# Three transformer blocks in one kernel: beta folded into the delta rule's decay, and each attention as one loop

## The chip, the cores and the metric

The kernel runs on one core of one Trainium2 chip. The metric is the device time of one launch in microseconds. All data and all matrix products are fp32.

## The reference, cut to what matters

Sequence 512, model width 1024, one batch. The first block mixes with a gated delta rule and a spatial gating unit, and then runs a mixture of 16 experts. The second block has two layers, each an attention (a forget-gate attention called FOX, then a latent attention with rotary keys called MLA) and a mixture of experts.

```python
# gated delta rule, 8 heads of 128
k_beta, v_beta = k * beta, v * beta
decay = where(causal, exp(g_cum[t] - g_cum[s]), 0)
a_mat = where(strict, (k_beta @ k.T) * decay, 0) + eye
u = solve(a_mat, v_beta)
w = solve(a_mat, k_beta * exp(g_cum))
v_new = u - w @ state
out   = (q * exp(g_cum)) @ state + ((q @ k.T) * decay) @ v_new
state = state * exp(g_last) + (k * exp(g_last - g_cum)).T @ v_new
# attention, 16 heads; cum only in FOX (head width 64), MLA has width 96 for q and k, 64 for v
s = q @ k.T * scale + cum[t] - cum[s]          # causal mask
o = softmax(s) @ v
# c @ w_ada: one row times 1024 x 6144, for each of the two layers
```

## The kernel before, in words

The program is a row of stages. A stage is a block: each engine has its own list of instructions in it, and the next stage begins when all engines and the queue of SP have come to the end of theirs. Inside a stage the engines wait for each other by named steps (`PE.wait(act, "sums")`: ScalarE waits until TensorE has done the step `sums`). There are 128-row tiles of the sequence, `T` = 4 of them, and 8 banks of PSUM of 512 fp32 columns.

Weights come through a ring of four SBUF slots (`Weights`), issued by SP in the order of use; a slot is loaded again when TensorE has finished with it. Beside the stages of the first block VectorE also sums `c @ w_ada` in *slabs*: SP loads 128 rows of `w_ada` (512 KB) into one of four buffers, VectorE multiplies and adds them into a 128 x 1024 accumulator, and after each 8 slabs SP stores the sum. `take_slabs` gives a stage its share. `project` (L343) is a general product stage: 8 jobs of 8 matmuls, the result of each drained by VectorE, with `slabs` spread evenly behind the jobs (`after`, L353). Its call at L796 (the product with `w_sgu_out`) has the last 12 slabs of a layer, so SP waits at its end for the last store.

The stage at L588 to L678 first multiplies the sequence by the 16 columns for a and b (L596 to L600: 4 tiles x 8 matmuls of 16 columns), then runs 16 jobs of the product for u and v. VectorE normalises q and k meanwhile, and ScalarE and VectorE make beta and the decay rate g from a and b.

The delta rule (L800 to L1030) works on chunks of 128 tokens, four rounds. In each round TensorE makes cumulative sums of g (`sums`), transposes q, k and k*beta (`qT`, `kT`, `kbT`), half of a product for the gate z, then `kk` (k against k*beta) and `qk`, the levels of a blockwise inverse of the unit triangular matrix (`t0`, `lev`, `dinv`, `turn`), and the products with the state. GpSimd makes k*beta and v*beta and k*decay. VectorE makes the differences of g for the decay (`diff`, `clip`), copies the identity into `inv_t` (`eye`), drains `kT`. ScalarE takes the exponentials and drains `qT` and `kbT`.

`attention` (L1977) is called for FOX (L2367) and MLA (L2741). For each group of 8 heads it has two stages: one that transposes all q and k of the group (64 transposes, L2006; ScalarE and VectorE take them to SBUF, L2013 and L2019), and the loop over 32 units (head h, tile t) in which the scores S (L2071), the transposes of the exponentials (L2079) and the products with v (L2089) run interleaved with lags of 3 and 4 units. In FOX the negative cumulative log-forget is a further row of the transposed keys, against a row of ones in q: it is transposed in the stage before (`cumT`, L2222 and L2298) and moved there by one DMA for each head (L2040), and rows 64 to 95 are padded. The row sums of the softmax come from the exponential's accumulator (L2102). After both groups `transpose_stage` (L254) turns the output. Bank use in the loop: four for S, two for the turned exponentials, two for the output.

Of the kernel before, what the change touches and what calls it, by code (L numbers as in the profile page):

```python
# [116 lines left out]
def build(nc, D, OUT, stop=None):  # L117
# [19 lines left out]
    with ctx:  # L137
# [205 lines left out]
        def project(srcT, kblocks, widths, by, drain, mids=0, slabs=0, first=None):  # L343
# [9 lines left out]
            after = lambda j: beside[j * slabs // len(jobs):(j + 1) * slabs // len(jobs)]  # L353
# [226 lines left out]
        a_in, g_all, beta_all, tmp_a, tmp_b = (sc[:, 288 + 32 * i:288 + 32 * (i + 1)] for i in range(5))  # L580
        ssq = [buf[6][:, 2304 + 32 * i:2304 + 32 * (i + 1)] for i in range(2)]
        square = [buf[6][:, 0:DM], buf[6][:, DM:2 * DM]]
        def th(a):
# [6 lines left out]
                    ["dt", "neg", "low", "high", "rate", "g"] + [("unit", i, t) for t in range(T) for i in range(2)])  # L590
        ac_names = ["beta", "exp", "rate"] + [(s, i) for i in range(2) for s in ("log", "inv")] + ["log"] + [("drained",) + j for j in jobs]
        stage(["ab"] + [("sum",) + j for j in jobs], ac_names, dv_names + slab_names(beside))
        with nc.Block() as block:
            @block.tensor
            def _(pe):
                for t in range(T):  # L596
                    for k in range(KD):
                        last = nc.tensor.matmul(bank[0][:, t * 2 * H:(t + 1) * 2 * H], featT[:, k, t * P:(t + 1) * P],
                                                ab_w[:, k, :], start=(k == 0), stop=(k == KD - 1))
                PE.done(last, "ab")  # L600
                for j, (n, t) in enumerate(jobs):
# [7 lines left out]
                    PE.done(last, ("sum", n, t))  # L609
                    if t == T - 1:  # L610
                        W.mark_used(ids[n], PE.sem, PE.value(("sum", n, t)))

            @block.vector
            def _(dve):
# [12 lines left out]
                AC.wait(dve, "beta")  # L627
                DV.done(nc.vector.tensor_tensor(th(a_in), ab[:, :, 0:H], bcast(dt_bias.unsqueeze(1), P, T, H), ALU.add), "dt")
# [24 lines left out]
            def _(act):  # L653
                ab = bank[0][:, 0:T * 2 * H].rearrange("p (t n) -> p t n", t=T)
                PE.wait(act, "ab")
                AC.done(nc.scalar.activation(th(beta_all), ab[:, :, H:2 * H], ACT.Sigmoid), "beta")
                nc.scalar.preload_act_table_set("natural_log_exp_and_others")
                DV.wait(act, "low")
# [144 lines left out]
        qkbT = buf[3][:, 0:2048].rearrange("p (h i n) -> p h i n", h=H, i=2)  # L803
        kT, decT = heads(buf[3][:, 2048:3072]), heads(buf[3][:, 3072:4096])
        qk, negT, inv_t, inv = (heads(buf[5][:, i * DM:(i + 1) * DM]) for i in range(4))
        lev, kb0, kd, vnew = (heads(buf[4][:, i * DM:(i + 1) * DM]) for i in range(4))
        kbs = [kb0, heads(ring[2][:, 0:DM])]
        gcol, gtot = sc[:, 448:456], sc[:, 456:464]
        e_g, e_tot, e_rest, b_eg = (sc[:, 464 + 8 * i:472 + 8 * i] for i in range(4))
# [6 lines left out]
        pe_n = (["sums", "qT", "kT", "kbT", "z"] + [("kk", u) for u in units] + [("qk", h) for h in halves] + [("t0", u) for u in units] +  # L816
                [(s, l, h) for l in LV for s in ("lev", "dinv") + (("turn",) if l < NL - 1 else ()) for h in units] +
                [(s, h) for s in ("ks", "qs") for h in halves] + [("vn", h) for h in halves] + [(s, h) for s in ("o", "s") for h in halves])
        ac_n = (["g", "e", "rest", "decay", ("qT", 0), ("qT", 1), ("kbT", 0), ("kbT", 1), "z"] + [("t0", u) for u in units] +
                [(s, l, h) for l in LV for s in ("lev",) + (("turn",) if l < NL - 1 else ()) for h in units] + [("vn", h) for h in halves])  # L820
        dv_n = (["rest", "beg", ("diff", 0), ("diff", 1), "clip", "eye", ("kT", 0), ("kT", 1)] + [(s, u) for u in units for s in ("neg", "first")] +
                [("qk", h) for h in halves] + [("add", l, h) for l in LV for h in units] +
                [(s, h) for h in halves for s in ("rk", "r")] + [(s, h) for h in halves for s in ("oq", "o", "sg", "s")])
        po_n = ["kb", "vb", "kd", "causal"]
# [7 lines left out]
        with nc.Block() as block:  # L832
            @block.tensor
            def _(pe):
# [6 lines left out]
                for c in range(T):  # L841
                    g_c = g_all[:, c * H:(c + 1) * H]
                    kb = kbs[c % 2]
# [29 lines left out]
                    for h in halves:  # L873
                        for j in range(HH):
                            last = nc.tensor.matmul(bank[5 + h][:, j * P:(j + 1) * P], kT[:, HH * h + j, :], qkbT[:, HH * h + j, 0, :], start=True, stop=True)
# [1905 lines left out]
```

## Time and profile before

| | |
|---|---|
| runs | 2282.35 us median of 3 (2280.46 to 2284.82) |
| profiled execution | 2285.79 us, of which the span of the trace 2283.8 us |
| TensorE matmul busy | 2138.2 us, 94% of the span |
| VectorE, ScalarE, GpSimd busy | 919.9, 525.1, 141.7 us |
| mean DMA rate | 164 GB/s |

Times in rows are microseconds from the start of the span unless marked ns. A row of the timeline has start, duration, engine, line of the kernel, operation, what it writes and reads, how many instructions were merged into the row, and in brackets the idle time of the engine just before and what ended it. An fp32 matmul is two instructions in the trace, a transpose is one. A releaser like "PEq L358" is the sequencer at a stage's boundary. The duration of a merged row runs to the last result, about 0.16 us after the engine could take the next instruction.

### The profile page before, as it was taken

What the parts mean: (1) busy time and instruction counts of PE and PEld (TensorE: products, weight loads), DVE (VectorE), ACT (ScalarE), POOL (GpSimd) and SP (SyncE); (2) the same over time, 40 slices, a digit from 0 to 9 for tenths busy, and PEclk for the clock granted to TensorE, in tenths of its full rate; (3) what the DMA queues carried; (4) which work ended last, traced back from release to release, by engine and by line L of the source; (5) the groups of instructions that cost most, each with busy time, mean ns of one, the idle gap of its engine ahead of it and who ended that gap; (6) DMA issues with size and microseconds to landing.
All of it is one profiled execution on the core that took longest, in us unless ns stands there. A gap on an engine that the chain in (4) does not pass through costs nothing. (4 is left out here: it accounts for less than half of the span.)

```text
span 2283.8 us, 21392 instructions
## 1 busy us (share of the span) xinstructions
PE 2138.2 (94%) x8144; PEld 1229.1 (54%) x8144; DVE 919.9 (40%) x1687; ACT 525.1 (23%) x1244; POOL 141.7 (6%) x201
## 2 busy tenths in 40 slices
PE   7999999989999999999799989999998989999994
PEld 4445445478884445444345468554444567654442
DVE  2446246344554024212355656342233467532223
ACT  1111011034332001111231146220003446411000
POOL 1000000011102000100100010000001000001001
PEclk9998999999999998999899999989998999989997
DMA  5333475420013224799626820149994120046995
GB/s 168 96 89 110 116 244 192 157 48 1 1 38 92 74 94 147 259 383 379 254 72 236 313 103 1 32 145 319 379 361 170 58 95 1 3 147 232 370 367 209
DMA packets 205258, 374.30 MB, mean 164 GB/s; under 512 B 21737, under 2 KB 123353, under 8 KB 204897
## 3 DMA queue, kind: packets, MB, share of 16 engines
q1 hardware_dynamic: 88080, 174.17, 23.4%
q10 hardware_dynamic: 105696, 157.30, 19.5%
q0 software_dynamic: 11376, 41.42, 4.8%
q8 instruction: 67, 1.10, 0.2%
q14 instruction: 39, 0.31, 0.0%
HBM read 329.31 MB, written 43.52 MB: 163 GB/s over the span
## 5 line engine op out<-in xcount | busy, mean ns | idle before, releaser
L1536 PE MATMUL bank<-ring,work 128*128 128x512 f32 x768 | 343.3, 601 | 11.4 <-issue 7.1
L1536 PEld LDWEIGHTS bank<-ring,work 128*128 128x128 f32 x768 | 144.1, 193 | 177.4 <-issue 177.4
L1547 PE MATMUL bank<-ring,work 128*128 128x512 f32 x384 | 173.0, 593 | 4.0 <-DVE work L1561 4.0
L2236 PE MATMUL bank<-ring,featT 128*128 128x512 f32 x384 | 170.8, 606 | 4.2 <-ACT featT L1925 2.6
L522 PE MATMUL bank<-featT,ring 128*128 128x512 f32 x384 | 168.7, 593 | 1.0 <-PEq L244 1.0
L1279 PE MATMUL bank<-ring,work 128*128 128x512 f32 x384 | 166.5, 593 | 3.1 <-PEq L244 3.1
L1558 DVE TENSOR_TENSOR work<-work,bank 128x256 f32<-128x256 f32 x48 | 20.2, 421 | 300.4 <-ACT work L1555 300.4
L2236 PEld LDWEIGHTS bank<-ring,featT 128*128 128x128 f32 x384 | 74.3, 195 | 96.0 <-issue 94.2
L1279 PEld LDWEIGHTS bank<-ring,work 128*128 128x128 f32 x384 | 72.3, 190 | 91.2 <-issue 91.2
L522 PEld LDWEIGHTS bank<-featT,ring 128*128 128x128 f32 x384 | 71.2, 190 | 82.0 <-issue 82.0
L608 PE MATMUL bank<-ring,featT 128*128 128x512 f32 x256 | 112.9, 605 | 0.0
L370 PE MATMUL bank<-ring,work 128*128 128x512 f32 x256 | 110.3, 593 | 2.0 <-PEq L697 1.0
L1547 PEld LDWEIGHTS bank<-ring,work 128*128 128x128 f32 x384 | 69.5, 190 | 74.9 <-issue 74.9
L1555 ACT ACTIVATE work<-bank 128x256 f32<-128x256 f32 x48 | 18.4, 383 | 394.5 <-PE bank L1536 394.5
L2071 PE MATMUL bank<-work 96*128 96x128 f32 (+3 forms) x256 | 96.2, 467 | 9.4 <-DMA work<-work 6.1
L1068 PE MATMUL bank<-ring,featT 128*128 128x512 f32 x192 | 85.0, 602 | 3.6 <-PEq L832 3.6
L2089 PEld LDWEIGHTS bank<-work,featT 128*128 128x128 f32 x640 | 81.5, 192 | 10.1 <-ACT featT L2102 8.1
L2089 PE MATMUL bank<-work,featT 128*128 128x64 f32 x640 | 86.5, 266 | 0.3
L1712 POOL DMA_INDIRECT work<-x_rows,ismall x48 | 45.1, 941 | 653.7 <-PE bank L1531 417.1
L608 PEld LDWEIGHTS bank<-ring,featT 128*128 128x128 f32 x256 | 49.7, 195 | 62.4 <-issue 62.4
L370 PEld LDWEIGHTS bank<-ring,work 128*128 128x128 f32 x256 | 48.5, 190 | 63.2 <-issue 63.2
L1566 DVE TENSOR_TENSOR work<-bank,work 128x512 f32<-128x512 f32 x64 | 41.2, 685 | 89.7 <-PE bank L1547 89.7
(426 smaller groups left out, 2928.6 us busy)
## 6 DMA issues: line engine op xcount, KB each, us to landing
ring<-in_w_in SPq DMA_DIRECT2D x16, 2048.0 KB, 13.3
ring<-in_moe_w_gate ACTq DMA_DIRECT2D x28, 1024.0 KB, 8.7
ring<-in_moe_w_up ACTq DMA_DIRECT2D x28, 1024.0 KB, 11.4
ring<-in_moe_w_down ACTq DMA_DIRECT2D x28, 1024.0 KB, 10.1
ring<-in_w_ada SPq DMA_DIRECT2D x48, 512.0 KB, 6.6
y_rows<-work ACTq DMA_DIRECT2D x48, 512.0 KB, 9.9
ring<-in_expert_w_gate ACTq DMA_DIRECT2D x14, 1024.0 KB, 9.2
ring<-in_expert_w_up ACTq DMA_DIRECT2D x14, 1024.0 KB, 11.8
```

The source lines that it names most:

```text
L370: last = nc.tensor.matmul(b[:, 0:width], left(k, t), w[:, k, :], start=(k == 0), stop=(k == kblocks - 1))
L522: last = nc.tensor.matmul(bank[b % 4][:, :], w[:, k, (b % 4) * P:(b % 4 + 1) * P], featT[:, k, :], start=(k == 0), stop=(k == KD - 1))
L608: last = nc.tensor.matmul(uv_bank(j)[:, :], featT[:, k, t * P:(t + 1) * P], w[:, k, :], start=(k == 0), stop=(k == KD - 1))
L1068: last = nc.tensor.matmul(zg_bank(j)[:, :], featT[:, k, t * P:(t + 1) * P], w[:, k, :], start=(k == 0), stop=(k == KD - 1))
L1279: last = nc.tensor.matmul(bank[j % 4][:, :], outT[:, k, t * P:(t + 1) * P], w[:, k, :], start=(k == 0), stop=(k == KD - 1))
L1536: last = nc.tensor.matmul(bank[2 + par][:, :], xgT[par][:, k, :], w_gu[par][:, k, :], start=(k == 0), stop=(k == KD - 1))
L1547: last = nc.tensor.matmul(bank[5 + h][:, :], hT[par][:, k, :], w_dn[par][:, k, span(h)], start=(k == 0), stop=(k == KF - 1))
L1566: return nc.vector.tensor_tensor(out, bank[5 + h][:, :], g2row[:, span(h)], ALU.mult)
L1712: nc.gpsimd.indirect_dma_start(out=xg[par], out_offset=None, in_=x_rows[:, :], in_offset=bass.IndirectOffsetOnAxis(ap=slot_tok[:, e:e + 1] ...
L2071: PE.done(nc.tensor.matmul(bank[i % 4][:, 0:(t + 1) * P], turned[0][:, h, t * P:(t + 1) * P], turned[1][:, h, 0:(t + 1) * P], start=True, ...
L2089: last = nc.tensor.matmul(bank[6 + h % 2][:, t * DVH:(t + 1) * DVH], pT[j % 2][:, s, :], v[:, s, c:c + DVH], start=(s == 0), stop=(s == t))
L2236: last = nc.tensor.matmul(f_bank(j)[:, :], featT[:, k, t * P:(t + 1) * P], w[:, k, :], start=(k == 0), stop=(k == KD - 1))
```

## The change

It does five things.

1. `project`: the slabs are spread behind the first 6 of 8 jobs; the last two have none.
2. The a and b columns: 8 matmuls with the 16 columns as weights and 512 tokens moving (result 16 x 512), a copy to SBUF by ScalarE, and after job 0 of the u and v product four transposes back. Beta is clamped at 1e-30 and its logarithm taken; `beta_all` holds log beta from then on.
3. Delta rule: log beta is subtracted from the column side of the decay (`g_key = gcol - log beta`), in `diff` and in `rest`. k*beta, v*beta and `kbT` go; `kk` is k against k, its sign comes in `neg`, now a scalar_tensor_tensor. `eye` moves from VectorE to GpSimd. ScalarE drains `qT` ahead of `rest` and `decay`, and its table is loaded at the stage's start.
4. `attention`: one stage. A loop over 16 heads x 4 tiles in which the transposes of q and k of a later head and those of a finished pair of outputs are interleaved. All three go through one bank X (bank 3). S has three banks. Within an iteration the turn of exponentials comes ahead of S.
5. q, k and v carry a further column for each head (ones, the negative cumulative sum, ones), so that the transposes bring the row of the decay and the product with v brings the softmax's sum. In FOX rows are 65 and not 96, `cumT` and its DMAs go; in MLA only v has the column.

```diff
 project
-            after = lambda j: beside[j * slabs // len(jobs):(j + 1) * slabs // len(jobs)]
+            busy = len(jobs) - 2
+            after = lambda j: beside[min(j, busy) * slabs // busy:min(j + 1, busy) * slabs // busy]
 stage of a and b, TensorE
-                for t in range(T):
-                    for k in range(KD):
-                        last = nc.tensor.matmul(bank[0][:, t * 2 * H:(t + 1) * 2 * H], featT[:, k, t * P:(t + 1) * P],
-                                                ab_w[:, k, :], start=(k == 0), stop=(k == KD - 1))
-                PE.done(last, "ab")
+                for k in range(KD):
+                    last = nc.tensor.matmul(bank[0][0:2 * H, :], ab_w[:, k, :], featT[:, k, :], start=(k == 0), stop=(k == KD - 1))
+                PE.done(last, "ab_sum")
...
+                    if j == 0:
+                        AC.wait(pe, "ab")
+                        for u in range(T):
+                            last = nc.tensor.transpose(bank[0][:, u * 2 * H:(u + 1) * 2 * H], ab_rows[:, u * P:(u + 1) * P], ident[0:2 * H, 0:2 * H])
+                        PE.done(last, "ab")
 delta rule, TensorE
-                    PO.wait(pe, "kb", c)
-                    DV.wait(pe, ("diff", 1), c)
-                    for h in range(H):
-                        last = nc.tensor.transpose(bank[h // HH][:, (h % HH) * P:(h % HH + 1) * P], kb[:, h, :], ident[:, :])
-                    PE.done(last, "kbT")
...
-                    AC.wait(pe, ("kbT", 1), c)
+                    AC.wait(pe, ("qT", 1), c)
 delta rule, VectorE
-                        DV.done(nc.vector.tensor_tensor(decT[:, hs(h), :], b4(h), per_head(gcol[:, hs(h)], HH), ALU.subtract), ("diff", h))
+                        DV.done(nc.vector.tensor_tensor(decT[:, hs(h), :], b4(h), per_head(g_key[:, hs(h)], HH), ALU.subtract), ("diff", h))
 delta rule, GpSimd
-                    if c >= 2:
-                        PE.wait(pool, ("vn", 1), c - 2)
-                    PO.done(nc.gpsimd.tensor_tensor(kbs[c % 2], k_c, per_head(be_c), ALU.mult), "kb")
-                    PO.done(nc.gpsimd.tensor_tensor(v_c, v_c, per_head(be_c), ALU.mult), "vb")
+                    if c:
+                        PE.wait(pool, ("vn", 1), c - 1)
+                    PO.done(nc.gpsimd.tensor_copy(inv_t, bcast(ident[:, :].unsqueeze(1), P, H, P)), "eye")
 attention, the places of the new steps in the loop of i, and its TensorE part
+            N_S = 3
+            TURN_LAG, PV_LAG = 3, 4
+            AHEAD = TURN_LAG - 1
+            q_at = {T * (h - 2) + 3: h for h in range(2, NHB)}
+            k_at = {T * (h - 1): h for h in range(2, NHB)}
+            o_at = {T * h + 8: h for h in hd}
+            out_turn_at = {T * h + 10: h // 2 for h in range(1, NHB, 2)}
...
+                    for i in range(END):
+                        if i in q_at:
+                            if q_at[i] >= 5 and q_at[i] % 2:
+                                pe.wait_ge(AC.sem, AC.value(("out", (q_at[i] - 5) // 2)))
+                            else:
+                                AC.wait(pe, ("q", 0))
+                            if q_at[i] > 2:
+                                pe.wait_ge(DV.sem, DV.value(("k", q_at[i] - 1)))
+                            turn_head(X, q, q_at[i], ("q", q_at[i]))
+                        if i in k_at:
+                            pe.wait_ge(AC.sem, AC.value(("q", k_at[i])))
+                            turn_head(X, k, k_at[i], ("k", k_at[i]))
+                        if i in out_turn_at:
+                            p = out_turn_at[i]
+                            DV.wait(pe, ("o", 2 * p + 1))
...
+                        if TURN_LAG <= i < N + TURN_LAG:
...
+                            for s in range(units[j][1] + 1):
+                                last = nc.tensor.transpose(bank[4 + j % 2][:, s * P:(s + 1) * P], sx[j % 4][:, s * P:(s + 1) * P], ident[:, :])
+                            PE.done(last, ("turn", j))
+                        if i < N:
...
+                            if i >= N_S:
+                                AC.wait(pe, ("exp", i - N_S))
+                            qT, kT = turned[h % TURNED_HEADS]
+                            PE.done(nc.tensor.matmul(bank[i % N_S][:, 0:(t + 1) * P], qT[:, t * P:(t + 1) * P], kT[:, 0:(t + 1) * P], start=True, stop=True), ("S", i))
 and its VectorE part
+                    for i in range(END):
+                        if i in k_at:
+                            keep_k(X, k_at[i])
+                        if i < N:
...
+                        if i in o_at:
 calls
-        oT2 = attention(FD, 0, 4096, 8192, 3 * 4096, None, k_gain, cumT)
+        oT2 = attention(FW, *qkv_f, 3 * QKV, 4 * 4096, None, k_gain)
```

ScalarE's part of the loop takes, at iteration i, the exponential of unit i, then the copy of q or of an output pair that TensorE makes at iteration i + 2, then the copy of the turned exponentials of unit i - 1.

## Rows read from the trace of the kernel before

**Rows 1.** Page, part 1: busy us, share of the span, instructions.
```profile
PE 2138.2 (94%) x8144; PEld 1229.1 (54%) x8144; DVE 919.9 (40%) x1687; ACT 525.1 (23%) x1244; POOL 141.7 (6%) x201
```

**Rows 2.** Windows: length, busy PE, PEld, DVE, ACT, POOL; PEclk, DMA share, GB/s.
```profile
202.00:215.80 13.80, 13.56 (x64) 13.59 (x64) 13.36 (x12) 1.28 (x1) 0.00 (x0) 0.50 0.79 248
...
216.00:226.00 10.00, 10.00 (x18) 4.29 (x18) 8.65 (x15) 4.05 (x11) 0.00 (x0) 0.72 0.00 0
```

**Rows 3.** Timeline of TensorE, the a and b columns and job 0.
```profile
202.24 13.80 PE L598 MATMUL bank<-work,featT 128*128 128x16 f32 x64 [0.94 <-PEq L504]
215.88 6.51 PE L608 MATMUL bank<-ring,featT 128*128 128x512 f32 x8
```

**Rows 4.** Timeline of VectorE, the end of the product with w_sgu_out.
```profile
455.66 0.69 DVE L797 TENSOR_TENSOR work<-bank,work 128x512 f32<-128x512 f32 x1 [4.98 <-PE bank L370]
456.27 2.66 DVE L323 SCALAR_TENSOR_TENSOR ring<-ring,ismall 128x1024 f32<-128x1024 f32 x2
```

**Rows 5.** Timeline of SP's queue, the layer's last store.
```profile
459.02 0.33 SPq L303 DMA_DIRECT2D ada_part<-ring  x1
```

**Rows 6.** Timeline of TensorE, first round of the delta rule.
```profile
462.57 3.76 PE L849 MATMUL bank<-tri,small 128*128 128x128 f32 x16 [6.95 <-PEq L358]
...
470.35 1.06 PE L861 MATMUL bank<-ident,work 128*128 128x128 f32 x8 [1.33 <-DVE work L969]
471.25 7.03 PE L839 MATMUL bank<-ring,featT 128*128 128x512 f32 x16
478.12 1.95 PE L871 MATMUL bank<-work 128*128 128x128 f32 x16
```

**Rows 7.** The same, second round.
```profile
523.15 2.05 PE L849 MATMUL bank<-tri,small 128*128 128x128 f32 x16
...
526.31 1.04 PE L856 MATMUL bank<-ident,work 128*128 128x128 f32 x8
527.64 1.06 PE L861 MATMUL bank<-ident,ring 128*128 128x128 f32 x8 [0.29 <-DVE work L969]
...
532.14 2.05 PE L871 MATMUL bank<-work 128*128 128x128 f32 x16
```

**Rows 8.** Lines by form: count, then busy us, mean ns of one, idle before.
```profile
L2119 DVE TENSOR_TENSOR bank<-bank,featT 128x128 f32<-128x128 f32 x128 | 38.0, 297 | 44.8 <-PE bank L2071 43.3
...
L767 DVE SCALAR_TENSOR_TENSOR work<-bank,small,work 128x128 f32<-128x128 f32 x32 | 8.5, 340 | 0.0
```

**Rows 9.** Timeline of GpSimd, second round (k times decay).
```profile
526.61 1.90 POOL L1025 TENSOR_TENSOR work<-work,small 128x1024 f32<-128x1024 f32 x1 [38.43 <-PE bank L853]
```

**Rows 10.** Timeline of VectorE, second round (clip).
```profile
527.53 1.53 DVE L971 TENSOR_SCALAR work<-work 128x1024 f32<-128x1024 f32 x1
```

**Rows 11.** Timeline of TensorE, FOX attention.
```profile
1330.49 7.15 PE L2006 MATMUL bank<-ident,work 128*64 128x128 f32 x64 [0.96 <-PEq L2191]
1343.72 4.51 PE L2071 MATMUL bank<-work 96*128 96x128 f32 x8 [6.09 <-DMA work<-work]
...
1353.82 0.44 PE L2071 MATMUL bank<-work 96*128 96x128 f32 x2
...
1359.32 0.44 PE L2071 MATMUL bank<-work 96*128 96x128 f32 x2
...
1450.31 41.44 PE L1279 MATMUL bank<-ring,work 128*128 128x512 f32 x96 [1.05 <-PEq L244]
```

**Rows 12.** The same, MLA attention.
```profile
1864.06 8.50 PE L2006 MATMUL bank<-ident,work 128*96 128x128 f32 x64 [5.51 <-PEq L2447]
...
1979.23 10.97 PE L1279 MATMUL bank<-ring,work 128*128 128x512 f32 x25 [1.05 <-PEq L244]
```

**Rows 13.** Lines by form of the attentions' copies (k, output, q).
```profile
L2134 DVE TENSOR_TENSOR work<-bank,small 128x256 f32<-128x256 f32 x32 | 13.6, 424 | 12.3 <-PE bank L2089 9.3
...
L2019 DVE TENSOR_SCALAR work<-bank,small 64x512 f32<-64x512 f32 x16 | 11.9, 744 | 10.1 <-PE bank L2006 8.3
...
L2013 ACT ACTIVATE work<-bank 64x512 f32<-64x512 f32 x16 | 9.5, 591 | 7.5 <-PE bank L2006 7.5
```

More of the change, by code:

```diff
@@ L654, in _ @@
                 ab = bank[0][:, 0:T * 2 * H].rearrange("p (t n) -> p t n", t=T)
+                PE.wait(act, "ab_sum")
+                AC.done(nc.scalar.activation(ab_rows, bank[0][0:2 * H, :], ACT.Copy), "ab")
                 PE.wait(act, "ab")
@@ L979, in _ @@
                         PE.wait(dve, ("kk", u), c)
-                        DV.done(nc.vector.tensor_tensor(negT[:, two, :], bank[UNIT_BANK[u]][:, 0:HU * P].rearrange("p (h n) -> p h n", h=HU),
-                                                        decT[:, two, :], ALU.mult), ("neg", u))
+                        DV.done(nc.vector.scalar_tensor_tensor(out=negT[:, two, :], in0=bank[UNIT_BANK[u]][:, 0:HU * P].rearrange("p (h n) -> p h n", h=HU),
+                                                               scalar=-1.0, in1=decT[:, two, :], op0=ALU.mult, op1=ALU.mult), ("neg", u))
                         DV.wait(dve, ("neg", u), c)
+                        PO.wait(dve, "eye", c)
                         DV.done(nc.vector.copy_predicated(inv_t[:, two, :], bcast(level_mask[:, 0, :].bitcast(I32).unsqueeze(1), P, HU, P),
@@ L2137, in attention @@
-            oT2 = work[:, qT_at:qT_at + KD * S].rearrange("p (k s) -> p k s", k=KD)
-            transpose_stage(k[:, :, 0:DM], oT2)
-            return oT2
+            o_pair = T4(scr[:, 6 * BANK:7 * BANK], P)
+            turned = [[work[0:dk, turned_at + (2 * i + m) * S:turned_at + (2 * i + m + 1) * S] for m in range(2)] for i in range(TURNED_HEADS)]
+            outT = work[:, out_at:out_at + KD * S].rearrange("p (k s) -> p k s", k=KD)
+            mx, inv = small[:, 64:128], small[:, 128:192]
@@ new lines, in attention @@
+            hd = range(NHB)
+            units = [(h, t) for h in hd for t in range(T)]
+            N = len(units)
+            N_S = 3
[5 more added lines that the diff above has]
+            out_turn_at = {T * h + 10: h // 2 for h in range(1, NHB, 2)}
+            END = max(out_turn_at) + 1
+            X = bank[3]
@@ L2217, in running_sums @@
                     PE.done(last, "cum")
-                def turn_sums():
-                    AC.wait(pe, "cum")
-                    for t in range(T):
-                        last = nc.tensor.transpose(bank[0][0:NHB, t * P:(t + 1) * P], f_cum[:, t * NHB:(t + 1) * NHB], ident[:, :])
-                    PE.done(last, "cumT")
                 def job(j):
@@ L2359, in _ @@
                 cb_a.gather(pool)
+                PE.wait(pool, ("sum",) + jobs[7])
+                PO.done(nc.gpsimd.memset(qkv_f[0][:, :, :, FD], 1.0), "ones_q")
+                PO.wait(pool, "ones_q")
+                PO.done(nc.gpsimd.memset(qkv_f[2][:, :, :, FD], 1.0), "ones_v")
             @block.sync
```

368 lines of the change are left out of this document (171 added, 197 removed).

## The prediction, made before the changed kernel ran

> **What bounds the kernel now.** I read the page's busy shares first: TensorE is busy 94% of the span, no other engine above 40% [rows 1], so a part of the change is worth what it takes out of TensorE's queue, plus the idle time in front of TensorE that it closes, plus what TensorE loses while its granted clock is low. The windows by stage came second; they show where that clock is down. In the stage of the a and b columns TensorE is busy for nearly all of 13.8 us at a granted clock of 0.50, its lower level, and in the 10 us from 216 on, with products 512 columns wide, the mean is 0.72 [rows 2]. Third, TensorE's timeline at the stage borders: it waits 6.95 us before the delta rule [rows 6], 6.09 us in the FOX attention for the DMA of the decay rows [rows 11], 5.51 us before the MLA attention [rows 12]; the other borders here cost about 1 us. Inside the attention loops there is no gap: a head follows the one before after 5.50 us (1353.82 to 1359.32) [rows 11]. Last, the timelines of VectorE and SP for what ends the waits.
>
> **a and b.** Before: 202.24 to 215.88 are 13.64 us, and job 0 behind it starts at the low clock: 10 us at 0.72 lose 2.8 us [rows 2, 3]. Together 16.4 us. After: 8 products of 512 columns, the shape of the z product, 6.87 us at full clock (471.25 to 478.12) [rows 6], and four transposes, 0.44 us (below). The form with 16 columns as weights is not in the trace; a weight load has less to load, not more, so I take z's price. What is lost at the low clock is 2.8 us if the clock rises as late as from 216 on, 1.35 us if as in MLA (8.50 against 7.15 us for 64 transposes) [rows 11, 12]; I take 2.1. After is then 9.4 us: **7.0 us less**. Bounds: the low clock all through makes 13.7 + 0.44 + 2.8 = 17.0 us (0.6 us worse), none of it 7.3 us (9.1 better). ScalarE's copy between lies under job 0, the new clamp and logarithm (64 of 128 columns or fewer) under job 1, since TensorE has seven banks ahead. The slabs of this stage are issued behind weight loads that wait for jobs 3, 7 and 11; they move with TensorE.
>
> **The slabs' tail.** TensorE ends the product at 455.62 (462.57 less 6.95), VectorE drains until 456.35, then sums two slabs until 458.93, SP stores at 459.02, and the store's landing lets the next stage start at 462.57 [rows 4 to 6]. After, the last slab is due behind job 5, two jobs of 6.87 us sooner, so the drain ends the stage: 456.35 and 0.35 us of border (the FOX border is 0.96 us with a drain of about 0.6 in it [rows 11]) make 456.7. **5.9 us less**. The last four slabs now follow a weight load of 2 MB more closely; they would have to come 10 us late to take it back, which would leave 0.
>
> **Delta rule.** With a gap of 1.1 us and not 6.95 the stage starts at full clock: from its start to the end of `kT` round one takes 6.45 us (469.02), round two 4.20 us (527.35) [rows 6, 7]: **2.25 us less**, bounds 0 and 2.25. Round one loses the wait of 1.33 us and `kbT`'s 0.90 us [rows 6]: **2.2 us**; its wait for z's end stays, and the table load falls ahead of it. In rounds two to four `kk` starts at 532.14; without `kbT`, half of z (3.44 us) starts at 526.31 + 0.87 and ends at 530.62 [rows 6, 7], and `qT` and `kT` are drained by then, because `eye` and `kbT` no longer stand ahead: 1.5 us each, **4.5 us**. `neg` as a scalar_tensor_tensor costs 340 against 297 ns on the nearest pair [rows 8]; 16 of them are 0.7 us, partly in the slack ahead of `t0`, so 0.3 us back; bounds 0 and 0.7. `eye` on GpSimd is not in the trace: one pass over 1024 columns, at most the 1.90 us of a product there [rows 9]. It starts when `vn` of the round before is done, some 13 us before anything asks for it. Price nothing; if it got in VectorE's way at the round's end, 1.9 us in each of three rounds. Stage and tail: 5.9 + 2.25 + 2.2 + 4.5 - 0.3 = 14.5 us.
>
> The rule that speaks against this edit: `clip` takes 1.53 us and ends 0.55 us after the GpSimd product that began ahead of it (526.61 + 1.90 = 528.51) [rows 9, 10]. The Trainium skill, "SBUF — State Buffer", section "Who interferes with whom", says that VectorE in a two-port mode, or with two SBUF inputs against a reading GpSimd instruction, is locked out until that one ends; the trace agrees with it here. By it the state update (two SBUF inputs) would stand still while `eye` runs, if they met; that is the fourth rival.
>
> **FOX, the stage before.** `cumT`'s four transposes go: **0.4 us**.
>
> **FOX attention.** Before: 1330.49 to 1450.31, 119.8 us [rows 11]. A transpose is (7.15 - 0.16)/64 = 0.109 us, four 0.44. After, on TensorE:
> - 16 transposes of heads 0 and 1, then S of unit 0 after the copy of k: 1.9 us;
> - 16 heads of 5.50: 88.0 us. Rows of 65 and not 96, and 65 output columns for 64, cost nothing: 128 columns of output per transpose cost 0.109 us, and the product with 64 columns runs no faster per instruction;
> - 14 heads x 8 transposes: 12.2 us; 8 output pairs x 0.44: 3.5 us;
> - waits for X. At the iteration where k is turned, VectorE has k's copy (0.744), mask (0.297), maximum (as the mask, 0.3), reciprocal (0.17, a small one) and output (0.424) [rows 8, 13]; begun 0.65 us after k's turn begins it has the output some 2.5 us after that point. TensorE wants it after its own 0.44 and the two short iterations (t of 0 and 1 in S and v, 1.87 of a head's 5.50 by TensorE's timeline between 1353.82 and 1359.32), at 2.3: 0.2 us, 7 times, 1.4 us. The first k: 0.15;
> - the end: lags running dry 0.6, the last pair waits 0.9 for its output, result 0.16, ScalarE's copy 0.6, border 0.3: 2.6 us.
>
> Sum 109.7 us: **10.1 us less**. The other chains have room. q's copy (0.59 on ScalarE) lies between its turn and k's, under one turn of exponentials (0.11), S of t = 3 (0.91) and the product with v of t = 3 (0.84), 1.86 us of TensorE's work. The tightest is turned exponentials of t = 1, their copy, the exponential of t = 3, its turn: about 1.45 us in 1.87.
>
> **MLA attention.** Before: 1864.06 to 1979.23, 115.2 us [rows 12]. After: the same 109.7, + 1.35 us of low clock at its start, + 0.2 us for each of 7 outputs since VectorE has `scaled` too, + 0.4 at the start: 112.8 us, **2.4 us less**.
>
> **Sum.** 7.0 + 14.5 + 0.4 + 10.1 + 2.4 = 34.4 us. The profiled execution took 2285.79 us, 2.0 us around its span of 2283.8; it would take 2251.4. The runs' median stands 3.4 us under it, at 2282.35, and goes to **2248 us**. With the terms' bounds and waits for X between 0 and double, 2243 to 2256.
>
> **The rivals.**
> 1. *One bank for three hand-overs (slower).* X passes 36 times in each attention from TensorE to a copying engine and back. If the copies lie open, each costs 0.59 to 0.744 [rows 13] and 0.2 us of signals: 28 of q, 28 of k, 16 of outputs make about 61 us, less the 4 counted, so 2305 us. From 0.48 us for each of the 72 the gain is gone. For it: one bank, and ScalarE and VectorE serve it in their queues behind exponentials and masks. Against: the order puts 1.86 us of products between q's turn and k's.
> 2. *The loop loses half a microsecond a head* in the queues of VectorE or ScalarE, now with 0.59 and 0.744 us more for each head: 32 x 0.5 = 16 us, 2264 us. Against: VectorE then has about 4.6 to 5 us of work in 6.6.
> 3. *The clock stays low*, through all of a and b and at the delta rule's start: 7.6 + 2.25 us, 2258 us. For it: TensorE was busy throughout and still at 0.50 [rows 2]. Against: behind it 512 columns brought the clock up.
> 4. *`eye` meets the state update*: 3 x 1.9 = 5.7 us, 2254 us.
> 5. *More*: no waits for X (2.8 + 0.6 us) and the clock up at once (2.1): 2243 us.
>
> **How the numbers follow.** Forecast 0.58; rival 1: 0.07 (0.04 of it beyond its point, 0.03 about at it); rival 2: 0.13; rival 3: 0.10; rival 4: 0.03; rival 5: 0.09. A measurement of this kernel tells 0.2%, 4.6 us, from no change. All but rival 1 are faster: 0.93, same 0.03, slower 0.04. The range 2240 to 2266 holds all but rival 1 and the outer ends of 2 and 5.
>
> **What would show it.** a and b at about 7 to 9 us with a rising clock; the delta rule starting about 1 us after the product before it, with `kk` about 11 us into round one; no `kbT`, `kk` 7.5 us after `sums` begins; each attention one unbroken loop of 6.6 us a head, with a gap of 0.2 to 0.4 us in front of each output turn. Wrong if gaps stand in front of the turns of q or k, if the slabs still end the product stage, or if a head takes over 7 us.

## The result, and the profile after

The changed kernel takes 2244.2 us (median of 4 runs, 2239.2 to 2249.0) against 2282.2 us before (4 runs). The ratio is 0.9832, 95% interval 0.9808 to 0.9856: 38 us less, where 2248 us was forecast (34.4 us less). In a later set of 5 runs it took 2242.8 us, ratio 0.9824 [0.9809, 0.9839]. The profiled execution took 2245.36 us with a span of 2243.4. The page's busy line answers to [rows 1]:

```profile
PE 2118.6 (94%) x8064; PEld 1210.7 (54%) x8064; DVE 906.9 (40%) x1677; ACT 510.1 (23%) x1117; POOL 123.3 (5%) x198
```

TensorE still bounds it at the same share. Its busy time is 19.6 us less; the span is 40.4 us less, so the other half of the gain is idle time of TensorE that is gone. Where that was is read from TensorE's timeline, one part at a time.

**a and b** (against [rows 3]). Columns of a timeline: start us, us, engine, line, operation, out<-in, shapes, count [idle before <- releaser].

```profile
202.06 9.09 PE L599 MATMUL bank<-featT,work 128*16 128x512 f32 x16 [0.94 <-PEq L505]
211.08 7.13 PE L608 MATMUL bank<-ring,featT 128*128 128x512 f32 x16
218.14 0.42 PE L613 MATMUL bank<-ident,work 16*128 16x16 f32 x4
```

The product takes 9.02 us and not 13.64, and job 0 behind it is at full clock at once. The windows (columns as in [rows 2]) show a mean granted clock of 0.77 in the product: 0.50 from 202 to 206 us, 0.98 from 206 to 211. In the 13.8 us of the old form, with 16 columns moving, it stayed at 0.50.

```profile
202.06:211.08 9.02, 9.02 (x17) 1.69 (x17) 8.88 (x8) 0.00 (x0) 0.00 (x0) 0.77 0.77 210
211.08:218.14 7.06, 7.06 (x17) 2.96 (x17) 6.96 (x7) 1.87 (x2) 0.00 (x0) 1.00 0.50 203
```

**Slab tail and delta rule, first round** (against [rows 6]). The first row is the product with `w_sgu_out`, the second the delta rule's first. The idle time in front of that second row is 1.05 us where it was 6.95. There is no `kbT` row and no wait of 1.33 us in front of it.

```profile
393.80 56.87 PE L371 MATMUL bank<-ring,work 128*128 128x512 f32 x128 [1.05 <-PEq L707]
451.71 2.02 PE L857 MATMUL bank<-tri,small 128*128 128x128 f32 x16 [1.05 <-PEq L359]
...
455.72 7.03 PE L848 MATMUL bank<-ring,featT 128*128 128x512 f32 x16
462.59 1.95 PE L874 MATMUL bank<-work 128*128 128x128 f32 x16
```

**Second round** (against [rows 7]). `kk` starts 7.47 us after `sums` (507.62 to 515.09); before it was 8.99 (523.15 to 532.14). The count of the last row is cut by the end of the window shown, as is that of the last row of the next block.

```profile
507.62 2.05 PE L857 MATMUL bank<-tri,small 128*128 128x128 f32 x16
...
509.88 1.07 PE L861 MATMUL bank<-ident,work 128*128 128x128 f32 x8
510.78 1.04 PE L864 MATMUL bank<-ident,work 128*128 128x128 f32 x8
511.66 3.60 PE L848 MATMUL bank<-ring,featT 128*128 128x512 f32 x8
515.09 1.61 PE L874 MATMUL bank<-work 128*128 128x128 f32 x13
```

**FOX attention** (against [rows 11]): 107.83 us from 1307.45 to 1415.28, before 119.82. L2025 turns q or k, L2050 an output pair, L2078 is the product with v.

```profile
1307.45 1.93 PE L2025 MATMUL bank<-ident,work 128*65 128x128 f32 x16 [0.95 <-PEq L2203]
...
1329.51 0.60 PE L2025 MATMUL bank<-ident,work 128*65 128x128 f32 x4
...
1335.68 0.60 PE L2025 MATMUL bank<-ident,work 128*65 128x128 f32 x4
...
1342.64 0.60 PE L2025 MATMUL bank<-ident,work 128*65 128x128 f32 x4
...
1413.68 0.66 PE L2050 MATMUL bank<-ident,featT 128*128 128x128 f32 x4 [0.73 <-DVE featT L2143]
1415.28 2.05 PE L1277 MATMUL bank<-ring,work 128*128 128x512 f32 x2 [0.94 <-PEq L2020]
```

A head without an output takes 6.17 us (1329.51 to 1335.68), its own part 5.30 and the turns of q and k 0.87. A head with one takes 6.96 (to 1342.64): 6.17, the output's turn 0.44, and a gap of 0.35. MLA takes 111.37 us (1830.96 to 1942.33), before 115.17.

Stage by stage, from the start of one stage's first TensorE row to the next one's, these are the parts that add up to the change of the span of 40.4 us: a and b with its gate products 127.52 to 120.64; the norm behind it 70.69 to 71.10; product with `w_sgu_out` to the delta rule 62.12 to 57.91; delta rule 223.24 to 213.71; to the FOX attention 644.68 to 642.03; FOX 119.82 to 107.83; to MLA 413.75 to 415.68; MLA 115.17 to 111.37; the end 304.57 to 301.07; before a and b, 0.18 less. The stages whose code is the same (but for `cumT`'s four transposes ahead of FOX) moved by -3.5 to +1.9 us. This is the clock: in the kernels below, with the same code in the stretch from FOX to MLA, its length lies between 410.8 us (`out_late`) and 415.8 us (`o_first`). TensorE's busy time in it is 387.8 and 392.8 us for the same instructions, so the whole difference lies in how long TensorE took for them. Of the 6.0 us by which this pair of executions beats the forecast of 34.4, 3.6 lie in such stages and 2.4 in the stages that were changed.

### The profile page after: what moved, and what is told of

Its sections match the earlier page's. It is cut to its first block and busy times, and to the rows that moved or that the text cites. A ratio compares the mean times of both kernels' runs of the same rounds, so it can differ in the third digit from the quotient of the medians.

```text
span 2243.4 us, 21072 instructions
## 1 busy us (share of the span) xinstructions
PE 2118.6 (94%) x8064; PEld 1210.7 (54%) x8064; DVE 906.9 (40%) x1677; ACT 510.1 (23%) x1117; POOL 123.3 (5%) x198
## 5 line engine op out<-in xcount | busy, mean ns | idle before, releaser
L2242 PE MATMUL bank<-ring,featT 128*128 128x512 f32 x384 | 169.7, 604 | 4.2 <-ACT featT L1923 2.6
L608 PE MATMUL bank<-ring,featT 128*128 128x512 f32 x256 | 110.4, 593 | 0.0
L2078 PEld LDWEIGHTS bank<-work,featT 128*128 128x128 f32 x640 | 88.6, 191 | 24.8 <-issue 14.4
L2070 PE MATMUL bank<-work 65*128 65x128 f32 (+7 forms) x256 | 89.7, 434 | 0.1
L1066 PE MATMUL bank<-ring,featT 128*128 128x512 f32 x192 | 83.3, 593 | 3.6 <-PEq L841 3.6
L2078 PE MATMUL bank<-work,featT 128*128 128x65 f32 x640 | 86.0, 265 | 0.1
## 6 DMA issues: line engine op xcount, KB each, us to landing
ring<-in_w_in SPq DMA_DIRECT2D x16, 2048.0 KB, 13.7
```

What stands on the lines that cost most here:

```text
L608: last = nc.tensor.matmul(uv_bank(j)[:, :], featT[:, k, t * P:(t + 1) * P], w[:, k, :], start=(k == 0), stop=(k == KD - 1))
L1066: last = nc.tensor.matmul(zg_bank(j)[:, :], featT[:, k, t * P:(t + 1) * P], w[:, k, :], start=(k == 0), stop=(k == KD - 1))
L2070: PE.done(nc.tensor.matmul(bank[i % N_S][:, 0:(t + 1) * P], qT[:, t * P:(t + 1) * P], kT[:, 0:(t + 1) * P], start=True, stop=True), ("S", i))
L2078: last = nc.tensor.matmul(bank[6 + h % 2][:, t * DVO:(t + 1) * DVO], pT[j % 2][:, s, :], v[:, s, h, :], start=(s == 0), stop=(s == t))
L2242: last = nc.tensor.matmul(f_bank(j)[:, :], featT[:, k, t * P:(t + 1) * P], w[:, k, :], start=(k == 0), stop=(k == KD - 1))
```

## The experiments

Each kernel's ratio is to runs of the kernel before on the same chip; the lengths are from its own trace.

**1 to 4. One part of the change at a time.** The edits are hunks of the diff shown above.

`slabs_only`:

```diff
-            after = lambda j: beside[j * slabs // len(jobs):(j + 1) * slabs // len(jobs)]
+            busy = len(jobs) - 2
+            after = lambda j: beside[min(j, busy) * slabs // busy:min(j + 1, busy) * slabs // busy]
```

> The kernel before with one part of the change: no slabs behind the last two jobs of the projections. Theory (the part is worth what it takes out in front of TensorE): the product with w_sgu_out, 455.62 to the delta rule's start 462.57, keeps a gap of about 1.1 us instead of 6.95 (5.9 us less), and the delta rule's first round, starting warm, is up to 2.25 us shorter; together 6 to 8 us less, about 2275 us. Rival (the slabs only move their wait): the last slabs come late behind the 2 MB weight load, the store still ends the stage, 0 to 1 us less.

Ratio 0.9966 [0.9956, 0.9977], 7.8 us less. The delta rule starts 57.92 us after the product before it, the rule takes 221.53 (1.71 less). The first round in its timeline:

```profile
456.97 2.02 PE L850 MATMUL bank<-tri,small 128*128 128x128 f32 x16 [1.05 <-PEq L359]
...
463.04 1.06 PE L862 MATMUL bank<-ident,work 128*128 128x128 f32 x8 [1.90 <-DVE work L970]
```

`kbT` starts 6.07 us after the stage and not 7.78: the warm start is worth 2.28 us up to `kT`'s end, but the wait for VectorE behind it grows from 1.33 to 1.90, since ScalarE's and VectorE's chain did not become shorter by as much. The change removes that wait as well. The gap of 6.95 became 1.05, 5.9 us as forecast, yet the stretch is only 4.2 us shorter: the product's start fell into a low clock, as in the trace of the whole change. A window at its start:

```profile
399.00:403.00 4.00, 3.95 (x6) 1.84 (x7) 0.00 (x0) 0.00 (x0) 0.00 (x0) 0.61 0.74 241
```

`ab_only` (weights of 16 columns, transposes; no clamp or logarithm of beta):

```diff
-                for t in range(T):
-                    for k in range(KD):
-                        last = nc.tensor.matmul(bank[0][:, t * 2 * H:(t + 1) * 2 * H], featT[:, k, t * P:(t + 1) * P],
-                                                ab_w[:, k, :], start=(k == 0), stop=(k == KD - 1))
+                for k in range(KD):
+                    last = nc.tensor.matmul(bank[0][0:2 * H, :], ab_w[:, k, :], featT[:, k, :], start=(k == 0), stop=(k == KD - 1))
```

> The kernel before with one part of the change: the a and b columns as 8 products of 512 columns with 16 columns as weights and four transposes, beta without clamp and logarithm. Theory: the stage's 13.64 us become about 9 us and the job behind it loses less at the low clock, together 7.0 us less, about 2275 us, and nothing else moves. Rival (clock): if the gain hangs on the clock alone and not on the fewer products, the granted clock of the stretch stays at 0.50, the stage takes 14 us and the gain is 0.

Ratio 0.9975 [0.9965, 0.9985], 5.7 us less. From the stage's start to the second job 17.0 us, and 121.2 us with all gate products. Over all kernels the stage is 126.5 to 127.5 us with the old form and 120.4 to 121.5 with the new one: 6.1 us on the mean. The rival, that only the clock pays, falls with the 9.69 us of this product.

`delta_only` (all edits of the delta rule, and the clamp and logarithm of beta):

```diff
-                    PO.wait(pe, "kb", c)
-                    DV.wait(pe, ("diff", 1), c)
-                    for h in range(H):
-                        last = nc.tensor.transpose(bank[h // HH][:, (h % HH) * P:(h % HH + 1) * P], kb[:, h, :], ident[:, :])
-                    PE.done(last, "kbT")
```

> The kernel before with one part of the change: beta taken into the decay in the delta rule (clamp and logarithm of beta added), no scaled keys or values, a and b columns and slabs as before. Theory: the border of 6.95 us in front of the delta rule and its cold first round stay; round one loses the wait of 1.33 us and kbT's 0.90, rounds two to four 1.5 us each: 6.5 us less, about 2276 us. In the changed kernel the rule took 9.5 us less than before, 2.25 of them put down to its warm start: here 7.3 us should be left by that, and 9.5 if the warm start is worth nothing.

Ratio 0.9971 [0.9962, 0.9981], 6.6 us less; the rule takes 215.92 us, 7.32 less, the 7.3 that were left for it. `kk` comes 13.10 us into the first round (before 15.55): 2.45 us. In the second:

```profile
519.23 2.05 PE L850 MATMUL bank<-tri,small 128*128 128x128 f32 x16
...
526.70 1.95 PE L867 MATMUL bank<-work 128*128 128x128 f32 x16
```

That is 7.47 us again, 1.52 less in each of three rounds. From one round's `kk` to the next it is 52.5 us where it was 54.1: the other 0.1 us of a round lies outside this stretch.

`attention_only` (one loop, rows of 65 with the decay as the last element):

```diff
-        oT2 = attention(FD, 0, 4096, 8192, 3 * 4096, None, k_gain, cumT)
+        oT2 = attention(FW, *qkv_f, 3 * QKV, 4 * 4096, None, k_gain)
```

> The kernel before with one part of the change: both attentions in one loop with one bank for the hand-overs, decay columns as rows of 65. The forecast's terms: 0.4 us in the stage before, 10.1 us in FOX, 2.4 us in MLA, together 12.9 us less, about 2269 us. By the changed kernel's trace: 0.4 + 12.0 + 3.8 = 16.2 us less, about 2266 us, if the surplus of 3.3 us belongs to the loop itself (each S product about 0.05 us shorter behind the turn of exponentials); 12.9 us if the surplus was only the difference of two executions.

Ratio 0.9936 [0.9916, 0.9956], 14.6 us less. FOX takes 107.82 us, MLA 111.27: 12.0 and 3.9 less, the same as in the whole change, so the surplus over the forecast is the loop's own. The four parts give 34.7 us together, the whole in the two sets 38 and 40. The intervals are 4 to 5 us wide for each of the first three parts and 9 us for the attentions, so the whole times neither show nor exclude that the parts help each other. The stages are sharper and show one such case: product and delta rule are 4.20 + 1.71 us less by `slabs_only` and 7.32 by `delta_only`, 13.23 together, and 13.74 in the first trace of the changed kernel, which had the same low clock. The 0.5 us is the wait for VectorE that grew in `slabs_only` and is gone with `kbT`.

**5. Where the attentions' surplus comes from.** In the trace after, S behind transposes is followed 0.05 us sooner than in the kernel before. `s_first` takes the changed kernel and puts S ahead of the turn:

```diff
-                pe_n += [("turn", i - TURN_LAG)] if TURN_LAG <= i < N + TURN_LAG else []
                 pe_n += [("S", i)] if i < N else []
+                pe_n += [("turn", i - TURN_LAG)] if TURN_LAG <= i < N + TURN_LAG else []
```

> The changed kernel with S ahead of the turn of the exponentials in TensorE's order. Theory (a transpose behind an S product costs TensorE less than S in front of transposes does, about 0.05 us for each of four S in a head, so the order alone gave 0.2 us a head): a head goes from 6.17 to about 6.37 us, both attentions together 6.4 us more, about 2251 us. Rival (the surplus has to do with rows of 65, the loop's unbroken course or the bank layout, not with the order): heads stay at 6.17 us and the time at 2244.

Ratio 0.983 [0.9815, 0.9845]; FOX 108.73 us, MLA 112.09: 0.90 and 0.86 more and not 3.2 each. In its timeline, the S of 512 columns behind the turn of q takes its old 0.86 us to the next row (1320.09 to 1320.95), that of 384 behind the product with v 0.70 (1317.89 to 1318.59), where it takes 0.65 in the changed kernel:

```profile
1317.89 0.86 PE L2060 MATMUL bank<-work 65*128 65x384 f32 x2
1318.59 0.60 PE L2069 MATMUL bank<-ident,featT 128*128 128x128 f32 x4
1319.03 0.78 PE L2078 MATMUL bank<-work,featT 128*128 128x65 f32 x6
1319.65 0.60 PE L2025 MATMUL bank<-ident,work 128*65 128x128 f32 x4
1320.09 1.02 PE L2060 MATMUL bank<-work 65*128 65x512 f32 x2
1320.95 0.27 PE L2069 MATMUL bank<-ident,featT 128*128 128x128 f32 x1
```

So it is what stands ahead of S that counts, not what follows it. The rows of the weight loads (PEld) show where the time goes; first `s_first` with S of 384 columns behind the product with v, then the changed kernel with it behind transposes:

```profile
1317.83 0.30 PEld L2060 LDWEIGHTS bank<-work 65*128 65x128 f32 x2
```

```profile
1321.17 0.30 PEld L2070 LDWEIGHTS bank<-work 65*128 65x128 f32 x2
1321.27 0.81 PE L2070 MATMUL bank<-work 65*128 65x384 f32 x2
1321.92 0.78 PE L2078 MATMUL bank<-work,featT 128*128 128x65 f32 x6
```

From the start of S's first weight load to the next row it is the same 0.76 us (1317.83 to 1318.59) and 0.75 us (1321.17 to 1321.92). But that load starts 0.06 us after the last product with v has started, and less than 0.01 us after the last transpose has (medians over the loops; 0.06 also in the kernel before). What holds the load back behind the product with v is open.

Two S of a head still stand behind transposes in `s_first`, those of q and k. The other two cost 0.10 us in each of the 8 heads without an output turn (6.27 us, 1315.63 to 1321.90, where it was 6.17), which makes 0.8; heads with an output turn stay at 6.97 us, since the gap in front of it takes the 0.10 up. My expectation had counted four S in every head.

**6. The same in the kernel before.** `turn_first` is the kernel before with the two orders exchanged in its attention loop, the reverse of the edit above, and nothing else.

> The kernel before with one edit in its attention loop: TensorE turns the exponentials of unit i - 3 ahead of S of unit i, not behind it; banks, rows and stages as before. Theory (an S product behind the product with v costs TensorE 0.05 us more than one behind transposes; all four of a head in the kernel before, two of a head where the turns of q and k stand ahead of the others): a head goes from 5.50 to 5.30 us, each attention 3.2 us less (119.8 to 116.6 and 115.2 to 112.0), together 6.4 us, about 2277 us. Rival (the surplus belongs to rows of 65, to the one bank, or is only how ends are modelled): the heads stay at 5.50 us and the time at 2283.

Ratio 0.999 [0.9981, 1.0]: 2.3 us less, between 0 and 4.3, and not the 6.4 expected. A head in the middle of the loop takes 5.30 us (1353.29 to 1358.59), as the theory said; [rows 11] had 5.50:

```profile
1353.29 0.39 PE L2073 MATMUL bank<-ident,featT 128*128 128x128 f32 x2
...
1358.59 0.39 PE L2073 MATMUL bank<-ident,featT 128*128 128x128 f32 x2
```

FOX as a whole takes 119.55 us, MLA 114.50. The two FOX loops are only 1.11 and 0.82 us shorter (46.75 and 44.92, before 47.86 and 45.74), not 1.6 each; MLA's are 0.69 each. The first turns now stand ahead of S and wait for exponentials while the loop fills, twice in an attention: from the first to the second head of the second FOX loop it is 2.91 us where it was 2.35. And 1.7 us of FOX's gain went again at the transposes behind the loop (5.35 against 3.69 us, mean clock 0.81 from 1440 to 1449), by the clock. The price per head is shown; the whole of 6.4 us did not come in that kernel.

**7 and 8. The gap in front of the output's turn.** Both start from the changed kernel. `o_first` gives VectorE the output ahead of k's copy, mask and maximum; `out_late` gives TensorE the output's turn behind that of the exponentials.

Each moves its step in the order of names and in the engine's loop; of `o_first` the first:

```diff
+                dv_n += [("inv", o_at[i]), ("o", o_at[i])] if i in o_at else []
                 dv_n += [("k", k_at[i])] if i in k_at else []
                 dv_n += ([("mask", i), ("neg", i)] + ([] if q_root is None else [("scaled", i)])) if i < N else []
-                dv_n += [("inv", o_at[i]), ("o", o_at[i])] if i in o_at else []
```

> The changed kernel with VectorE's output of a head (reciprocal and product) ahead of k's copy, mask and maximum of the same iteration. Theory (the gaps in front of the output turns, about 0.35 us in FOX and 0.55 us in MLA, 7 of each, are VectorE's order alone): they close, 5 to 6 us less, about 2238.5 us. Rival (k's copy, begun up to 0.6 us later, is then late for the bank of the hand-overs or for S): a gap of the same size opens in front of the next turn, 2244 us.

> The changed kernel with the output's turn behind the turn of the exponentials in TensorE's order. Theory: that turn (four transposes, about 0.5 us) covers the gap of 0.3 us in FOX and nearly that of 0.5 us in MLA: 4 to 5 us less, about 2239.5 us. Rival (ScalarE's copy of the exponentials now waits behind the copy of the output, which comes 0.5 us later, and the product with v waits for it): the gain is given back, 2244 us or more.

| kernel | median us | ratio to before | FOX us | MLA us |
|---|---|---|---|---|
| changed kernel, same set (`after_again`) | 2242.8 | 0.9824 [0.9809, 0.9839] | 107.83 | 111.23 |
| `out_late` | 2237.2 | 0.9797 [0.9783, 0.9810] | 105.53 | 108.33 |
| `o_first` | 2234.4 | 0.9784 [0.9770, 0.9797] | 105.53 | 107.57 |

Both are faster than the kernel before and, by the medians of one set of runs, 5.6 and 8.4 us faster than the changed one; by the stages 5.2 and 6.0 us. The expectations were 4 to 5 and 5 to 6 us. (The profiled execution of `o_first`, at 2240.3 us, was the slowest of its five, that of `after_again`, at 2238.6, the fastest, so their whole times can't be compared.) In `o_first` the two heads of a pair take 12.78 us (1330.32 to 1343.10), twice 6.17 and 0.44: no gap is left. k's copy, late by the 0.6 us of the output, makes nobody wait. `out_late` leaves 0.76 us more in MLA, where VectorE has `scaled` too.

```profile
1328.17 0.61 PE L2050 MATMUL bank<-ident,featT 128*128 128x128 f32 x4
1330.32 0.60 PE L2025 MATMUL bank<-ident,work 128*65 128x128 f32 x4
...
1340.95 0.61 PE L2050 MATMUL bank<-ident,featT 128*128 128x128 f32 x4
1343.10 0.60 PE L2025 MATMUL bank<-ident,work 128*65 128x128 f32 x4
```

`after_again`, the changed kernel unchanged, was the measure beside them:

> The changed kernel once more, as the measure for the three kernels beside it: 2244 us, the FOX attention 107.8 us, the MLA attention 111.4 us. The product with w_sgu_out started at a granted clock of 0.5 in the two kernels with the new slab order and at 1.0 in the four with the old one; if the slab order did that, it does so again here, if it was chance in the clock, it may not.

Here the product with `w_sgu_out` starts at full clock and the delta rule follows after 56.22 us, 5.90 less than before. With the new slab order 5 of 8 traces show 56.2 us and 3 show 57.9 (`slabs_only`, the first of the changed kernel, `eye_dve`); the five with the old order all show 62.1. TensorE's rows ahead of that start are alike in all of them, and the same kernel shows both. So within the new order it is chance in the clock, worth 1.7 us; whether that order makes it likelier, 8 and 5 traces don't settle.

**9 and 10. GpSimd and VectorE.** `rest_first` moves ScalarE's exponential for k's decay ahead of its copies of q, so that GpSimd's product with it starts earlier; `eye_dve` writes the identities on VectorE behind `clip`.

```diff
+                    DV.wait(act, "rest", c)
+                    AC.done(nc.scalar.activation(e_rest, e_rest, ACT.Exp), "rest")
                     PE.wait(act, "qT", c)
                     for h in halves:
                         AC.done(nc.scalar.activation(qT[:, hs(h), :], b4(3 + h), ACT.Copy), ("qT", h))
-                    DV.wait(act, "rest", c)
-                    AC.done(nc.scalar.activation(e_rest, e_rest, ACT.Exp), "rest")
```

```diff
                     DV.done(nc.vector.tensor_scalar(decT, decT, 0.0, None, ALU.min), "clip")
+                    DV.done(nc.vector.tensor_copy(inv_t, bcast(ident[:, :].unsqueeze(1), P, H, P)), "eye")
...
-                    PO.done(nc.gpsimd.tensor_copy(inv_t, bcast(ident[:, :].unsqueeze(1), P, H, P)), "eye")
```

> The changed kernel with ScalarE's exponential for k's decay ahead of its copies of q, as before the change. It lets GpSimd's product (two SBUF inputs, 1.9 us) start earlier and lie beside VectorE's clip. Theory (the clip's 1.53 us before and 0.69 us after are a lock-out by that product): the clip goes back to about 1.5 us in rounds two to four, kT's copies end about 0.8 us later, and the two kk-to-z slacks hide it or not: the delta rule takes 213.7 to 216 us. Rival (the clip is shorter because eye and the scaled keys are gone): it stays at 0.69 us.

> The changed kernel with the identities written by VectorE behind the clip, as before the change, and not by GpSimd. Theory (the move took a pass off VectorE in front of kT's copies): kT's copies come 0.6 to 0.7 us later, kk waits for them by up to 0.4 us in rounds two to four, and the delta rule takes 0 to 1.5 us more, 2244 to 2246 us. Rival (the eye on GpSimd disturbs the state update): the gap between the rounds becomes shorter by up to 1.9 us without it, 2239 us.

`rest_first`: one run, 2246.7 us, which alone says nothing of the time; the rule takes 213.81 us, 0.1 more. In its second round `clip` takes 1.61 us again (1.60 in the next two), beside a GpSimd product that began ahead of it; in the changed kernel (`after_again`) it takes 0.69, since that product begins later. VectorE of `rest_first`, and GpSimd behind it:

```profile
509.81 1.61 DVE L972 TENSOR_SCALAR work<-work 128x1024 f32<-128x1024 f32 x1
511.34 1.27 DVE L975 COPY work<-bank 128x512 f32<-128x512 f32 x2
```

```profile
508.98 1.90 POOL L1023 TENSOR_TENSOR work<-work,small 128x1024 f32<-128x1024 f32 x1 [10.41 <-ACT small L935]
```

The same of `after_again`:

```profile
508.75 0.69 DVE L972 TENSOR_SCALAR work<-work 128x1024 f32<-128x1024 f32 x1
509.36 1.28 DVE L975 COPY work<-bank 128x512 f32<-128x512 f32 x2
```

```profile
508.94 2.25 POOL L1023 TENSOR_TENSOR work<-work,small 128x1024 f32<-128x1024 f32 x1 [11.45 <-ACT small L938]
```

The copies out of PSUM (L975) take the same 1.28 us in both. `kk` hides the rest: it waits for z's half until 512.78, and the copies end at 512.61.

`eye_dve`: ratio 0.9853 [0.9835, 0.9872], the rule takes 218.00 us, 4.3 more, well above the 0 to 1.5 expected. The identities' copy, a pass of 0.68 us in the kernel before (first block), now begins behind the start of GpSimd's product (third block) and takes 2.39 (second block):

```profile
528.97 0.68 DVE L972 COPY work<-ident 128x1024 f32<-128x1024 f32 x1
```

```profile
511.60 2.39 DVE L973 COPY work<-ident 128x1024 f32<-128x1024 f32 x1
513.90 1.28 DVE L976 COPY work<-bank 128x512 f32<-128x512 f32 x2
```

```profile
511.18 2.25 POOL L1020 TENSOR_TENSOR work<-work,small 128x1024 f32<-128x1024 f32 x1 [43.37 <-ACT small L938]
```

`kk` then waits 1.2 us for VectorE in each of three rounds, 3.6 of the 4.3 us. With the copy at 0.68 us, `kT`'s copies would have ended at 513.5 (an estimate: 515.19 less 1.71), before z's half lets `kk` start at 513.96 (510.52 + 3.44); so it is the meeting that costs, not the pass. The expectation had counted the pass alone. On GpSimd the pass takes 1.04 us (496.46 to 497.50 in `after_again`), while VectorE has no work from 495.3 to 498.3. The rival of this run, that `eye` on GpSimd disturbs the state update, falls: the step from the state products to `sums` is 3.49 us with either (500.76 to 504.25, 503.00 to 506.49).

## Why the prediction was right

Right in sign, size and in nearly every step; it was 3.8 us too high in the first set of runs. That the sum came so near is in part luck: the two attentions gave 3.3 us more than forecast, the stages of the first block 0.9 us less in the first trace, and unchanged stages add several us of chance in either direction. By its own steps:

- *a and b*: 7.0 forecast. The product's end came at 9.02 + 0.42 us, 9.4 as in the working, but the 2.1 us of low clock lay inside the product (9.02 us at a mean of 0.77, 6.87 foreseen) and not behind it. Up to the second job it is 16.43 us (202.06 to 218.49) where it was 23.42 (202.24 to 225.66), 7.0 less; over the whole stage 6.1 on the mean of all traces. Where the other 0.9 us went is open.
- *Slab tail*: 5.9 forecast, 5.90 measured at full clock, 4.2 where the next start falls into a low clock.
- *Warm start*: 2.25 forecast, 2.28 shown by `slabs_only`.
- *Round one*: 2.2 forecast, 2.45; *rounds two to four*: 1.5 each, 1.52. *`neg`* cost nothing where 0.3 us was forecast: it takes 0.42 us for 128x256 before and after, and the 340 against 297 ns that it was priced by are of another pair of passes. Stage and tail: 14.5 forecast, 13.7 in the first trace and 15.5 in the second. *`eye` on GpSimd* at nothing was right, and rival 4 did not show: the two don't meet.
- *FOX attention*: 10.1 forecast, 12.0. The mis-sized term is "16 heads of 5.50": they are 5.30, because the new order puts transposes ahead of S (`s_first`, `turn_first`). The working had taken the old head over and given the new order no price. That is 3.2 us; the waits for the output, 0.35 and not 0.2 us, 7 times, and small ones at the ends take some back.
- *MLA attention*: 2.4 forecast, 3.8, by the same 3.2 us; its waits for X are 0.55 and not 0.4 us, and its start costs 0.8 us more than FOX's beside the low clock (2.37 us from the turn of q of head 2 to that of k, FOX 1.58), where 0.4 was put.
- *`cumT`*: 0.4 us forecast, not seen by itself. The stretch ahead of FOX is 642.6 to 647.3 us long in the five traces with its transposes and 641.9 to 644.5 in the eight without.
- *Rival 1* (one bank open to its hand-overs) fell: no gap stands in front of the turns of q or k within the loop. *Rival 2* fell with the head of 6.17. *Rival 3* fell in both places. *Rival 5*, 2243 us, came nearer than its chance of 0.09, but not by its reasons: the waits for X stayed.
- The Trainium skill, "SBUF — State Buffer", section "Who interferes with whom", says that VectorE with a two-port mode and GpSimd lock each other out. The trace agrees: `clip` takes 0.69 us free and 1.61 behind GpSimd's product, and the change takes that collision away by the order on ScalarE alone. Where GpSimd's product came second it took 2.25 us and not 1.90. In this kernel the lock-out is worth 0.1 us where z's products cover it (`rest_first`) and 4.3 us where they don't (`eye_dve`).

## What to carry to other kernels

Where one engine is busy 94% of the span, sum its queue stage by stage and take the borders from its own timeline: the idle times and waits read that way came out within 0.3 us each here. A loop whose order changes should not be priced by its old length: that step missed by 3.2 us in each attention. A wait on the bounding engine can hang on the order in the queue of another that is mostly idle: putting the older and shorter piece of work first there (`o_first`) gave 6 us by the stages, 8 by the medians, and cost only a change of order. When a pass is moved between VectorE and GpSimd, look which SBUF-to-SBUF pass of the other it lies beside, not only at how long it is.

## What the runs showed of the hardware that was not expected

- An S product (fp32, 128 to 512 columns) has the next row start 0.05 us later when it stands behind the product with v than behind transposes: 0.70 against 0.65 us for 384 columns, 0.49 against 0.44 for 256, 0.91 against 0.86 for 512. All of it lies in the start of S's own first weight load, 0.06 us after the last product with v has started and less than 0.01 us after the last transpose has; why the load starts later there is open.
- Only SBUF-to-SBUF passes of VectorE stood behind GpSimd's product; copies out of PSUM beside it kept 1.28 us for two (`after_again`). The lock holds the other way as well: where `clip` came first, the GpSimd product took 2.25 us and not 1.90.
- The granted clock fell to 0.5 (the 1.2 GHz level) at the start of the same product in 3 of 8 executions with nothing in TensorE's rows to tell them apart. Such chance moves single stages by 1 to 2 us and the stretch from FOX to MLA by 5, so a stage's length should be compared over several traces before a cause is looked for.
